# Reordering the linear-attention part: the next head's projections between the heavy steps of a head

## The reference, cut to what matters

```python
h = rmsnorm(x, norm_mix);  proj = h @ w_in        # qb, kb, vb, og, gf, gb, ma, mb, ...
logg = log_sigmoid(gf @ w_gate_f + b_gate_f) / 16  # and the same for gb: 16 gate inputs -> 128 per head
b = cumsum(logg, within a chunk)
q_in, k_in, k_out = q * exp(b), k * exp(-b), k * exp(b_last - b)
o_intra = tril(q_in @ k_in.T) @ v                  # inside a chunk
state = exp(b_last) * state + k_out.T @ v          # from chunk to chunk
o = o_intra + q_in @ state                         # forward + backward
ob = rmsnorm(o, gla_norm) * silu(og);  yb = ob @ w_proj_b
x = x + (sigmoid(ma) * ya + sigmoid(mb) * yb) @ w_out
```

## Time and profile before

| What | us |
|---|---|
| Three executions | 1423.12, 1430.71, 1430.9 (median 1430.71) |
| Profiled execution: span from first to last instruction | 1427.5 |
| ... its own time | some 3 more than its span, if it is one of the two at 1430.7 to 1430.9 (the list of times does not say which was profiled) |
| GLA heads (end of first `qkb` group after `vb` 0 to end of the last `heavy`) | 360.2 to 558.4 |
| `og` groups and `obT` | 558.4 to 635 |
| `ma` to `out`, router | 635 to 988 |
| Experts and end | 988 to 1427.5 |

### The profile page before, as it was taken

One profiled execution on the slowest core, in us unless ns is written; L12 is line 12 of the kernel. 1 busy time (PEld: TensorE's weight loads), 2 busy tenths in 40 slices (PEclk: granted clock), 3 DMA queues, 4 the chain that ended last, 5 costly groups with the idle time before them and its releaser, 6 DMA issues. The chain is left out here.

```text
span 1427.5 us, 19757 instructions
## 1 busy us (share of the span) xinstructions
PE 1235.1 (87%) x7936; PEld 1139.9 (80%) x7936; DVE 627.7 (44%) x1051; ACT 555.8 (39%) x905; POOL 446.3 (31%) x196
## 2 busy tenths in 40 slices
PE   6989999998899888999999998971889888988870
PEld 3988999797697877999999998961778878887860
DVE  5002111227435354541121132247477777766756
ACT  6223242344454352332122130151465666566632
POOL 2211120131120201221121242233466676666613
PEclk8999999998999999999999999985898999999995
DMA  7520001233111301202212214063598999999937
GB/s 250 163 60 30 30 9 41 85 91 109 46 45 46 89 1 49 62 23 87 67 38 75 66 61 151 31 212 134 165 335 286 329 310 341 317 321 318 341 137 265
DMA packets 158728, 200.39 MB, mean 140 GB/s; under 512 B 11625, under 2 KB 139773, under 8 KB 158654
## 3 DMA queue, kind: packets, MB, share of 16 engines
q1 hardware_dynamic: 151150, 183.41, 39.3%
q0 software_dynamic: 7504, 15.94, 3.2%
HBM read 179.32 MB, written 34.42 MB: 150 GB/s over the span
## 5 line engine op out<-in xcount | busy, mean ns | idle before, releaser
L837 POOL TENSOR_TENSOR w_lo<-raw,w_hi 128x2048 fp32r<-128x2048 f32 (+2 forms) x37 | 152.6, 4124 | 689.5 <-ACT w_hi L975 689.4
L1202 PE MATMUL bank<-hT_hi,w_hi 128*128 128x384 f32 (+1 forms) x592 | 203.6, 344 | 4.0 <-DVE hT_lo L1491 4.0
L1203 PE MATMUL bank<-hT_lo,w_hi 128*128 128x384 f32 (+1 forms) x592 | 200.7, 339 | 0.0
L1204 PE MATMUL bank<-hT_hi,w_lo 128*128 128x384 f32 (+1 forms) x592 | 200.5, 339 | 0.0
L896 POOL TENSOR_TENSOR lo_gate<-raw_gate,hi_gate 128x2048 fp32r<-128x2048 f32 x30 | 139.2, 4641 | 121.0 <-ACT hi_gate L964 120.8
L1202 PE MATMUL bank<-w_hi,hT_hi 128*128 128x256 f32 x528 | 158.5, 300 | 0.0
L1204 PE MATMUL bank<-w_hi,hT_lo 128*128 128x256 f32 x528 | 156.6, 297 | 0.0
L1203 PE MATMUL bank<-w_lo,hT_hi 128*128 128x256 f32 x528 | 156.6, 297 | 0.0
L1748 DVE TENSOR_TENSOR lo_up<-raw_up,hi_up 128x2048 fp32r<-128x2048 f32 x31 | 109.0, 3516 | 53.6 <-ACT hi_up L964 53.5
L1202 PEld LDWEIGHTS bank<-hT_hi,w_hi 128*128 128x128 f32 (+1 forms) x592 | 111.8, 189 | 8.5 <-DVE hT_lo L1491 4.4
L975 ACT ACTIVATE w_hi<-raw 128x2048 fp32r<-128x2048 f32 (+2 forms) x42 | 74.0, 1763 | 103.7 <-PE bank L1204 103.7
(11 more groups left out here) (285 smaller groups left out, 2895.3 us busy)
## 6 DMA issues: line engine op xcount, KB each, us to landing
raw_gate<-in_w_exp_gate SPq DMA_DIRECT2D x32, 1024.0 KB, 7.7
raw_up<-in_w_exp_up SPq DMA_DIRECT2D x32, 1024.0 KB, 10.8
raw_down<-in_w_exp_down SPq DMA_DIRECT2D x32, 1024.0 KB, 6.0
raw<-in_w_in SPq DMA_DIRECT2D x25, 1024.0 KB, 6.0
y_d<-m_y SPq DMA_DIRECT2D x32, 512.0 KB
y_d<-zeros SPq DMA_DIRECT2D x11, 512.0 KB, 7.2
raw<-in_w_in SPq DMA_DIRECT2D x8, 512.0 KB, 5.9
raw<-in_w_proj_b SPq DMA_DIRECT2D x4, 1024.0 KB, 5.0
```

The source lines that it names most:

```text
L837: pool.tensor_tensor(w_lo[:, g % 2, 0:kb, 0:n], raw[:, g % 2, 0:kb, 0:n], w_hi[:, g % 2, 0:kb, 0:n].bitcast(F32), ALU.subtract).then_inc(w ...
L1202: pe.matmul(out, l_hi, r_hi, start=j == 0, stop=False)
L1203: pe.matmul(out, l_hi, r_lo, start=False, stop=False)
L1204: ins = pe.matmul(out, l_lo, r_hi, start=False, stop=j == n - 1)
```

## The change

The list of steps is written in another order, and what this needs in buffers is added:

- `decay` is cut into four steps: `soft` (ACT: Abs, Exp, Ln), `cumul` (DVE: minimum, scans), `decay` (ACT: the two exponentials and the chunk decays), `decay2` (the rest).
- The four `z` steps of head `h + 1` stand ahead of `heavy(h)`. `soft`, `cumul` and `decay` of head `h + 1` stand between the steps of `heavy(h)`, and so do the 6 `vb` tiles of head `h + 1`. `decay2` of head `h + 1` stands behind, and then the `qkb` group of head `h + 2`. Behind `decay2` of the last head stands `og` 0, and `og` 1 stands between the steps of the last `heavy`.
- `vb` gets a second buffer, in the part of `o_gla` that belongs to the last head. The gates of `og` 0 and 1 are kept in the freed `vb` and `qkb` buffers; `sg` has four tiles.
- The multiplication of norm and gate is a step of its own, `ob`. It stands with the tiles of `og` 2 and 3, and the transposes stand between the blocks of `ma` 0 and `mb` 0.

No instruction of the computation is added or removed.

```diff
-    def chain(h):
-        r = [S(kind="z", h=h, d=d, s=s) for d in range(2) for s in range(2)] if h else []
-        return r + [S(kind="decay", h=h)]
...
+    steps += [S(kind=k, h=0) for k in ("soft", "cumul", "decay", "decay2")] + proj("qkb", 1)
     for h in range(GH):
-        steps += chain(h)
-        if h:
-            steps += proj("vb", h)
+        r = heavy(h)
         if h + 1 < GH:
-            steps += proj("qkb", h + 1)
-        steps += heavy(h)
+            steps += [S(kind="z", h=h + 1, d=d, s=s) for d in range(2) for s in range(2)]
+            r = r[0:3] + [S(kind="soft", h=h + 1)] + r[3:13] + [S(kind="cumul", h=h + 1)] + r[13:25] + [S(kind="decay", h=h + 1)] + r[25:]
+            steps += interleave(r, proj("vb", h + 1))
+            steps.append(S(kind="decay2", h=h + 1))
+            steps += proj("qkb", h + 2) if h + 2 < GH else proj("og", 0)
+        else:
+            steps += interleave(r, proj("og", 1))
     steps.append(S(kind="gstat"))
-    for h in range(GH):
+
+    obT = lambda h: [S(kind="obT", h=h, i=i) for i in range(NT)]
+    for h in (2, 3):
         r = proj("og", h)
-        steps += r[:NT] + [S(kind="obT", h=h, i=i) for i in range(NT)] + r[NT:]
+        for i in range(NT):
+            steps += [r[i], S(kind="ob", h=h, i=i)]
+            if i % 2:
+                steps.append(S(kind="ob", h=0, i=3 * (h - 2) + i // 2))
+        steps += r[NT:]
+    steps += interleave([S(kind="ob", h=1, i=i) for i in range(NT)] + obT(0) + obT(1) + obT(2) + obT(3), proj("ma", 0) + proj("mb", 0))
...
-        vb = at("vb", [P, NT, DV], F32, 154)
+        vb0 = at("vb", [P, NT, DV], F32, 154)
+        vb = [vb0[:, :, :], o_gla[:, :, (GH - 1) * DV:GH * DV]]
+        og_kept = [at("og0", [P, NT, DV], F32, 154), at("og1", [P, NT, DV], F32, 148)]
...
-        sg = at("sg", [P, 2, DV], F32, 188)
+        sg = at("sg", [P, SGR, DV], F32, 203)
```

More of the change, by code:

```diff
@@ L43 @@
 WRING = 3
+SGR = 4
 OVER = 11
@@ L276, in plan @@
     for n, s in enumerate([s for s in steps if s.kind == "o"]):
+        s.seq = n
+    for n, s in enumerate([s for s in steps if s.kind == "ob"]):
         s.seq = n
@@ L1024, in _ @@
                         elif name == "vb":
-                            act.activation(vb[:, s.i, :], src, ACT.Copy).then_inc(act_evac, 1)
+                            act.activation(vb[a % 2][:, s.i, :], src, ACT.Copy).then_inc(act_evac, 1)
                         else:
[L1027 to L1030, removed]
+                            n = NT * (a - 2) + s.i
+                            if a == 1:
+                                need(act, E_, ko, 2 * 2 + 2)
+                            if n >= SGR:
+                                need(act, E_, ob_done, find(kind="ob", h=2 + (n - SGR) // NT, i=(n - SGR) % NT)[0].seq + 1)
+                            act.activation(og_kept[a][:, s.i, :] if a < 2 else sg[:, n % SGR, :], src, ACT.Silu)\
+                               .then_inc(act_evac, 1)
                 elif k == "sc":
@@ L1066, in _ @@
                                    bias=gate_bias[:, s.d, s.h:s.h + 1]).then_inc(act_evac, 1)
-                elif k == "decay":
+                elif k == "soft":
                     h = s.h
@@ L1079, in _ @@
                         act.activation(et[:, d, :], et[:, d, :], ACT.Ln, bias=1.0).then_inc(softplus, 1)
+                elif k == "decay":
+                    h = s.h
                     for d in range(2):
@@ L1084, in _ @@
                         act.activation(dec[:, h % 2, d, :], last, ACT.Exp, scale=1.0 / 16).then_inc(e1, 1)
+                elif k == "decay2":
+                    h = s.h
                     for d in range(2):
@@ L1208, in _ @@
                 k = s.kind
-                if k in ("w", "norm", "natural", "comb", "mix", "decay", "gstat", "mixT", "norm2", "route", "place"):
+                if k in ("w", "norm", "natural", "comb", "mix", "soft", "cumul", "decay", "decay2", "ob", "gstat", "mixT", "norm2", "route", "place"):
                     continue
@@ L1304, in _ @@
                     rows = slice(CH * (c % 2), CH * (c % 2) + CH)
-                    ins = pe.matmul(b_[:, 0:DV], kot[rows, s.d * NT + c // 2, :], vb[rows, c // 2, :],
+                    ins = pe.matmul(b_[:, 0:DV], kot[rows, s.d * NT + c // 2, :], vb[s.h % 2][rows, c // 2, :],
                                     start=True, stop=True)
@@ L1326, in _ @@
                             parts.append((half, q_in[:, 1, tok], st[:, 1, nch - 2 - c, :]))
-                    pe.matmul(b_[:, 0:DV], ptg[:, it.seq % 2, :], vb[:, s.i, :], start=True, stop=False,
+                    pe.matmul(b_[:, 0:DV], ptg[:, it.seq % 2, :], vb[s.h % 2][:, s.i, :], start=True, stop=False,
                               skip_group_check=True)
@@ L1332, in _ @@
                 elif k == "obT":
-                    need(pe, E_, ob_done, NT * s.h + s.i + 1)
+                    need(pe, E_, ob_done, find(kind="ob", h=0, i=s.i)[0].seq + 1 if s.h == 0 else GH * NT)
                     for c in range(2):
@@ L1441, in link @@
                 settle()
+            chunks = lambda x: x.rearrange("p (c t) -> p c t", t=CH)
             wide = lambda x, n: x.rearrange("p (i o) -> p i o", o=1).broadcast_to([P, NT, n])
@@ L1445, in _ @@
                 k = s.kind
-                if k == "ts" and s.dest[0] == "og":
-                    h, i = s.dest[1], s.i
+                if k == "ob":
+                    h, i = s.h, s.i
                     x = o_gla[:, i, h * DV:(h + 1) * DV]
                     link(dve.scalar_tensor_tensor(x, x, grstd[:, i, h:h + 1], g_gla[:, :], ALU.mult, ALU.mult))
-                    evac_done(dve, E_, s.job)
-                    dve.tensor_tensor(x, x, sg[:, (NT * h + i) % 2, :], ALU.mult).then_inc(ob_done, 1)
+                    evac_done(dve, E_, find(kind="ts", dest=("og", h), i=i)[0].job)
+                    gate = og_kept[h][:, i, :] if h < 2 else sg[:, (NT * (h - 2) + i) % SGR, :]
+                    dve.tensor_tensor(x, x, gate, ALU.mult).then_inc(ob_done, 1)
                     continue
@@ L1566, in _ @@
                     dve.tensor_tensor(o0, o0, o2, ALU.add).then_inc(oa_done, 1)
-                elif k == "decay":
+                elif k == "cumul":
                     h = s.h
-                    q, kk = qkb[h % 2][:, 0, :], qkb[h % 2][:, 1, :]
-                    chunks = lambda x: x.rearrange("p (c t) -> p c t", t=CH)
                     for d in range(2):
@@ L1577, in _ @@
                         dve.tensor_tensor_scan(x, scan_mask[:, :], x, 0.0, ALU.mult, ALU.add).then_inc(cum, 1)
+                elif k == "decay2":
+                    h = s.h
+                    q, kk = qkb[h % 2][:, 0, :], qkb[h % 2][:, 1, :]
                     for d in range(2):
```

2 lines of the change are left out of this document (1 added, 1 removed).

## The result

The changed kernel took **1471.54 us** (median of four, 1468.39 to 1482.14) against 1426.91 for the kernel before, measured beside it: **1.0319 times as long, 95% interval 1.0278 to 1.0361**. The time lies 7.5 us above the forecast of 1464 and inside its range of 1447 to 1475. The rise was forecast as 33 us and measured as 45 between the medians, 39 between the two profiled spans.

The account below looks back on a forecast made before the run. PE was taken as the bound, nearly always busy in the GLA part, with some 21 us idle. Late gate weights +38.4, clock +10.5, first state -5.9 and interleaving -10 gave +33 on 1430.7: 1464 us, range 1447 to 1475.

Parts of the forecast that it names:

- The late `wgate`: Before `z`, PE waits in three heads for gate weights issued late on POOL: +38.4 us, bounds 34.5 and 41.1.
- The clock: Behind each wait, `z` runs at the 1.2 GHz level: 3.5 us per head, +10.5 in all; bounds 1.6 and 4.5.
- The first state: Between transposes and first state, heads 0 to 2 wait less for ACT's `w_hi`, 0.75 us left each: -5.9 us.
- The interleaving: In `heavy`, `vb` tiles between the steps remove mask waits and state lag: -10 us, between 4 and 14 won.
- lag of the states: In `heavy`, first-sequence states take longer per pass; interleaving wins back 1.3 us a head, 5 in four.
- hold by `cumul`: In `heavy`, `cumul` on DVE delays masks and `o`: 1 us for each of three heads; bounds nothing and 5.2 a head.
- The first, ready gate weights: Rival: `wgate` lands before `z` needs it, so only the 16 us of gains remain, 1415 us; chance 0.03.
- The second: Rival: waits before `z` are cheap, landings near 3.9 us, low clock cost, full `heavy` gain: 1450 us; chance 0.10.
- The third: Rival: gating in the `og` groups falls behind, PE waits for two DVE locks, 2 x 3.9 us more: 1472; chance 0.09.
- The signs named in advance: Profile: three 11 to 14 us waits before half-clock `z`, `kot` wait 3 us in last head alone, mask waits at most 5.

Follow-up runs that it names:

- E1: Changed kernel, but POOL issues the next head's gate-weight load right after the last `z` of the head before: 1420.15 us, 0.9949 of the kernel before.
- E2: Kernel before, with only the four `z` steps of head `h + 1` moved ahead of `heavy(h)`: 1476.32 us, 1.0329 of the kernel before.
- E5: Changed kernel plus 64 unread products of the projections' kind before the first `z` of heads 1 to 3: 1466.94 us, 1.026 of the kernel before.
- E4: E1 with the `vb` and `og` 1 tiles as whole groups behind `heavy` again: 1441.98 us, 1.0106 of the kernel before.
- E3: Changed kernel plus 16 unread fp32 products before the first `z` of heads 1 to 3: 1464.14 us, 1.0256 of the kernel before.
- E6: E1 with the six tiles in three pairs between the `heavy` steps instead of singly: 1407.84 us, 0.9857 of the kernel before.

## Why the prediction was right, and where its terms were not

All terms are for the profiled executions: 353.74 - 311.78 = +42.0 for the GLA part. It begins 1.5 us earlier in the changed kernel, and about 1.6 us come back in the experts' part, which makes the 38.9 between the spans.

- **The late `wgate`: +38.4 forecast, 38.5 measured** (gaps before `z` of 11.67, 13.52 and 13.85 less the normal step between products; the view of waits has 38.0). E1 and E2 show it from both sides. Landings of 3.9, 5.6 and 6.1 us in the kernel before became 3.99, 5.84 and 6.18 from issue to `z`. The rule of the Trainium skill ("DMA: Bandwidth & Descriptors", section "Anatomy of one DMA — SWDGE (gpsimd) path"), about 2.0 us fixed, was off by 2 to 4 us for each; the rows decided rightly.
- **The clock: +10.5 forecast, 12.0 in the place named.** `z` takes 2.65 us more per head (5.49 - 2.84) and the transposes 1.35 more (2.82 - 1.47), three times 4.0. Two errors nearly cancel here, so that the term came out this close is partly luck. `z` was priced too high, 3.5 for 2.65: the 0.82 us per pass came from a row of two passes, and a row of two takes more per pass than one of eight at 2.4 GHz as well (0.91 us for two at 329.84, 0.455 each, against 0.355). The transposes stood only in the upper bound; they belonged in the sum. In head 1 the low level reached further, into the states and the first tile, which makes that `heavy` 40.16 us long instead of 38.21: 2 us more. E5 confirms by experiment that at least 8.3 us of the loss are clock.
- **The first state: -5.9 forecast, -5.8 measured.** 0.78 us are left before the first state in each of the three heads, 0.75 were forecast. In the last head the way from the end of the products to the first state shrank by 1.3 us, which wasn't foreseen (0.6 of it is the wait for `kot`, 0.4 a wait for `et`).
- **The interleaving: -10 forecast, -0.9 measured. This term failed.** The idle time did go (mask waits 10.0 to 2.9). Three things were wrong with the rest. First, the "lag of the states", 5 us, was no wait for DVE but the clock: the 0.178 us per pass in head 0 lay in a stretch at half clock (3.4 us from 365.73 on). Heads 1 and 3 have such a stretch too (from 427.17 and 536.39 on), while head 2 at 1.00 has 28 passes in 3.77 us, 0.135 each. The clock of these stretches wasn't read. From the first state to the first `o` in heads 0 to 3 of the kernel before (length, PE busy, clock, DMA share, GB/s), and head 2's states:

```profile
364.58:371.43 6.85, 6.07 (x37) 0.75 0.39 102
426.76:434.14 7.38, 6.07 (x36) 0.77 0.42 112
489.45:496.30 6.85, 4.86 (x37) 1.00 0.36 77
536.37:543.99 7.62, 6.06 (x36) 0.78 0.43 99
```

```profile
489.45 3.77 PE L1305 MATMUL bank<-vb,kot 64*128 64x256 f32 x28 [2.62 <-ACT kot L1093]
```

  Second, PE pays when its work alternates between the projections' products and the state products. The same states in the changed kernel, with the second tile between:

```profile
539.72 1.56 PE L1323 MATMUL bank<-vb,kot 64*128 64x256 f32 x10
541.21 0.38 PE L1220 MATMUL bank<-w_hi,hT_hi 128*128 128x256 f32 x1
541.43 0.28 PE L1221 MATMUL bank<-w_lo,hT_hi 128*128 128x256 f32 x1
...
544.07 0.28 PE L1222 MATMUL bank<-w_hi,hT_lo 128*128 128x256 f32 x1
544.28 1.56 PE L1323 MATMUL bank<-vb,kot 64*128 64x256 f32 x10
```

  The tile's first and last products hold PE for 0.22 and 0.21 us (541.21 to 541.43, 544.07 to 544.28), those between for 0.12, and ten passes (five states) take 1.49 us, 0.149 each, where head 2 before had 0.135. The busy time of a head rises by 1.75 us (35.78 to 37.53), where the prediction had it as constant. Third, the hold by `cumul`, 3 of the 5 us taken off in the sum, was no hold at all: in E4, without tiles beside it, PE stands 7.8 us for the mask in each of heads 0 to 2, and with them 0.2.
- **Sum:** 38.5 + 12.0 - 5.8 - 0.9 - 1.3 - 0.5 (shorter stretches from `og` 2 on) = +42.0, as in the two rows. The -0.9 runs from the first state to the end of the next group of products, over all four heads, and holds the head 1 rest of the clock. So the rise was forecast 9 us too small by the trace, nearly all of it the interleaving, and 11.6 too small between the medians. That the time missed by 7.5 us and not by 11.6 is luck: the forecast started from a median of 1430.71, and the kernel before had 1426.91 in the end.
- **The rivals.** The first, ready gate weights, is what E1 builds: 7 us below the kernel before where 16 were priced, and the 9 us that lack are the same wrong term for `heavy`. The second fell with its landings, two of which stayed near 6 us. The third did not come: between `gstat` and the first product on `obT` PE shows no wait but 0.8 us of issue, so the gating in two groups keeps up.
- **The signs named in advance** came as forecast, one apart: the `kot` wait is 2.5 us in the last head and 0.8 in the others rather than in the last alone.

## What to carry to other kernels

When a consumer moves forward, ask when its producer is issued, not only when its inputs are ready: here 8 KB loads issued behind a 4.5 us instruction made the change 3.2% slower, and moving their issue turned it into a gain of 0.5%. A wait on the pacing engine can cost more than its length: here the work behind it ran at half clock for 9 to 13 us. Fill waits with pairs of tiles where the wait is, not with single tiles everywhere, and look at which small products the cut takes apart (last section); and before a rate per pass is used as a term, read the granted clock of that stretch and of another head.

## What the runs showed of the hardware that was not expected

- Keeping PE busy through the wait didn't hold the clock. In E3 and E5 it worked at 1.00 through 10.5 to 11.3 us of filler, up to a gap of 0.5 to 3.2 us, and `z` and the transposes behind ran at 0.50 to 0.74 in five of six heads; in head 0 of E5, behind the shortest gap, they ran at 1.00. Even in E1, with no wait, the clock of that stretch in head 0 was 0.77:

```profile
361.19:367.21 6.02, 5.24 (x22) 3.50 (x21) 0.00 (x0) 5.89 (x10) 3.54 (x1) 0.77 0.00 0
```

  while the same stretch in heads 1 and 2 of E1 ran at 1.00 and took 5.89. What differs between these heads stays open.
- The low level outlasts the wait. In the changed kernel it lasted until 13.4 us after `z` had started in head 1, and 8.8 and 8.9 us in heads 0 and 2, though PE stood for only 0.8 us of them.
- Six tiles as pairs in three places cost PE nothing beside the group that they came from (34.90 us busy against 35.78), as single tiles in six places 1.75 us. Half as many changes give back all of it, and the states show part of the reason. In E6 the first ten states stand in a row:

```profile
426.92 2.43 PE L1324 MATMUL bank<-o_gla,kot 64*128 64x256 f32 x20 [1.58 <-ACT kot L1112]
429.28 0.39 PE L1221 MATMUL bank<-w_hi,hT_hi 128*128 128x256 f32 x1
```

  Their 20 passes take 2.36 us, 0.118 each, against 0.149 in the runs of ten above. In E6 the passes start two at a time, less than 0.04 us apart, and each two take 0.216 us. In the changed kernel the last two passes of the ten from 539.72 on start alone, 0.216 us apart. There the first state stands alone ahead of a tile and holds PE for 0.60 us (536.07 to 536.67); in the last head the first two states stand together and hold it for 0.63 (595.63 to 596.26). The kernel takes the chunk of a state from the upper or the lower 64 rows, and the two directions need opposite halves; so a tile behind an odd number of states seems to leave passes without a partner. Over a head the 40 state passes take 6.32 us in the change and 4.92 in E6, which is 1.4 of the 2.6 us of busy time between them. No run varied this alone.
- Between executions the part behind GLA varies by more than some of the effects told apart here: from the first product on `obT` to the end it is 743 us in the profiled run of E6 and 757 in that of E1, with the same code there. So spans of single executions were used only for stretches, and ratios of many runs for whole kernels.
